# A two-layer decoder step on one core: RMSNorm's factor applied at the PSUM read, split inputs cut chunk by chunk across the norm, prologue by chunks and tail by token tiles

## The chip, the core and the metric

The kernel runs on one core of a Trainium2 chip. TensorE (PE) does matmuls and transposes, VectorE (DVE) and ScalarE (ACT) the work between them, GpSimd (POOL) builds constants and starts some DMAs, SyncE (SP) starts most DMAs. Every engine has its own instruction stream and they meet at semaphores. The metric is the device time of one execution in microseconds (us); lower is better.

## The reference

One inference step of a two-layer trunk for 512 prompt tokens and 64 sample tokens (8 sequences of 8), model width 1024, everything in float32:

```python
def rms_norm(x, g):
    y = xf * lax.rsqrt(jnp.mean(xf * xf, axis=-1, keepdims=True) + EPS) * g
for layer in range(DEPTH):                     # DEPTH = 2
    h = rms_norm(x, g_mix[layer])
    mix = even_mixer(h, ...) if layer % 2 == 0 else odd_mixer(h, ...)
    x = x + mix
    h = rms_norm(x, g_mlp[layer])
    x = x + jnp.square(jax.nn.relu(h @ w_up[layer])) @ w_down[layer]
y = rms_norm(x, g_final)
```

A mixer is one input projection of h, an attention (forgetting in layer 0, stick-breaking in layer 1) beside a gated part, and one output projection. There are five norms: before each mixer, before each MLP, and the last one. The factor `rsqrt(mean)` is one number for each token; the gain `g` is one number for each feature.

## The kernel before

Activations lie feature-major: `X` is 128 partitions x 8 chunks (k) x 576 tokens, so a norm factor is a vector along the free axis, replicated on all partitions in `R` (128x576).

Every projection is cut into **units** of 128 output features. A unit multiplies a 1024x128 weight tile with 576 tokens: 8 chunks k, in each three products (high weight x high input, high weight x low input, low weight x high input; each float32 operand is split into a high part `WH`, `HH` and a low rest `WL`, `HL`), in each two halves of 288 tokens. That is 48 matmuls. Units are numbered through the program (188 of them), alternate between two weight buffers and, before, between PSUM banks 0,1 and 2,3. For unit g, SP loads `WR`, ACT makes `WH` (`cut_high`), DVE makes `WL` (`cut_low`), PE runs `unit`, then ACT and DVE read the banks: `evac_in` copies a projection (ACT one half, DVE the other), `evac_up` takes relu (ACT), squares (DVE), and splits into `ffH` (ACT) and `ffL` (DVE), `evac_add` adds to `X` (DVE), after which ACT squares the chunk and DVE sums it into `SQS`. The tile of a weight buffer can only be cut again when the unit two before has finished, and PE starts a unit only when both readers are done with its banks.

Between the last unit ahead of a norm and the first behind it stands `norm(z)`, z from 0 to 4: PE sums `SQS` over partitions (`rms`), DVE makes mean + EPS in `R`, ACT takes Ln and Exp, DVE multiplies each chunk by gain and `R` into `TMP`, ACT writes `HH`, DVE writes `HL`. `pair_after_norm` runs the first two units behind the norm together, chunk by chunk, as `HL` chunks come:

```python
def scale(k):
    ...
    V.scalar_tensor_tensor(dst, X[:, k, :], gain, R[:], ALU.mult, ALU.mult).then_inc(S["normed"], 1)
```

In the prologue PE waits for POOL's `consts`, transposes `XN` (tokens x features, one DMA) into `X`, and the first norm (z = 0) follows. In the tail (z = 4) the normed `Y` is transposed back in eight steps, copied to `XN` by DVE, and POOL stores it with two DMAs. The order of work on each engine is the order of the program text; there is no scheduler. MLP groups run in the order `MLP_ORDER`: up 0, up 1, down 0, up 2, down 1, up 3, down 2, down 3, eight units each.

Of the kernel before, what the change touches and what calls it, by code (L numbers as in the profile page):

```python
# [19 lines left out]
def trunk(nc, x_prompt, x_sample, cache_fox_k, cache_fox_v, cache_fox_logf, cache_sb_k, cache_sb_v, state_conv,  # L20
# [6 lines left out]
    ds = bass.ds  # L27
# [34 lines left out]
    with ctx:  # L62
# [31 lines left out]
        low_addr = h_addr + KT * T * 4  # L94
        mask_f = place("mask_f", [P, 3, 2, P], F32, low_addr)
# [3 lines left out]
        row_rep = place("row_rep", [2 * NT, NH, 2 * NT], F32, low_addr + 4096)  # L99
        row_neg = place("row_neg", [2 * NT, 2, 2, NT], F32, low_addr + 8192)  # L100
# [18 lines left out]
        ffL = [place(f"ffL{i}", [P, KT, T], F32R, arena + (i * 2 + 1) * KT * T * 4) for i in range(2)]  # L119
        at[0] = arena  # L120
# [64 lines left out]
        def sems(*names):  # L185
            for n in names:
# [4 lines left out]
             "consts", "zeroed", "vec_turned", "x_turned", "x_copied", "x_squared", "x_summed",  # L191
             "sum_step", "rms_sum", "rms_mean", "rms_ln", "rms_scale", "normed", "norm_high", "norm_low",
             "lf_turned", "lf_copied", "lf_suffix_step", "lf_suffixed", "lf_tail", "d_past",
             "wf_high", "wf_low", "f_logits", "f_copied", "f_turned", "f_biased", "f_abs", "f_exp", "f_ln", "f_logf", "F_sums", 
             "nbi_set", "relu_squared", "ff_high",
# [3 lines left out]
             "y_turned", "y_copied", "stored", "stored_kn")  # L199
# [11 lines left out]

        NORM_G = [0, 2 * KT, KT, 3 * KT, 4 * KT]
        CONV_V = 5 * KT

        def unit_loop(eng, body, g0, n, last_plain=False, first_plain=False, i0=0):
# [4 lines left out]
            for u in range(first):  # L220
                body(g0 + u, i0 + u, u, "second" if u == 0 else None)
# [117 lines left out]
        N_STORES = 3 + 2 + 2  # L339
# [7 lines left out]
        def _(sp):  # L347
            sp.dma_start(XN[:, 0:TT, :], x_prompt[0].rearrange("(i p) d -> p i d", p=P)).then_inc(S["x_in"], 16)
            sp.dma_start(XN[0:NS, TT, :], x_sample.rearrange("b t d -> (b t) d")).then_inc(S["x_in"], 16)
            sp.dma_start(pages[0:1, :], page_table.rearrange("(o a) b -> o (a b)", o=1)).then_inc(S["pt_in"], 16)  # L350
            sp.dma_start(vec_rows[0:2 * KT, :], g_mix.rearrange("l (k p) -> (l k) p", p=P)).then_inc(S["vec_in"], 16)
            sp.dma_start(vec_rows[2 * KT:4 * KT, :], g_mlp.rearrange("l (k p) -> (l k) p", p=P)).then_inc(S["vec_in"], 16)
            sp.dma_start(vec_rows[4 * KT:5 * KT, :], g_final.rearrange("(k p) -> k p", p=P)).then_inc(S["vec_in"], 16)
            sp.dma_start(vec_rows[5 * KT:n_vec, :], conv_w[0].rearrange("w (k p) -> (w k) p", p=P)).then_inc(S["vec_in"], 16)
# [18 lines left out]
            for L in range(2):  # L373
# [36 lines left out]
                for kind, grp in MLP_ORDER:  # L410
                    view = up_v[L] if kind == "up" else dn_v[L][grp]
                    unit_loop(sp, load_weights(view, grp * DM if kind == "up" else 0), g, KT)
                    g += KT
            sp.wait_ge(S["stored"], N_STORES * 16)
# [7 lines left out]
        def _(pool):  # L422
            g = nc.gpsimd
            for t in (ident, zero_col, head_rep, step_rep, row_rep, row_neg, mask_f):
                g.memset(t[:], 0.0)
# [3 lines left out]
            pool.wait_ge(S["zeroed"], 1)  # L429
            sel = g.affine_select  # L430

            def step(ins, n=[1]):
# [4 lines left out]
            sel(out=ident[:], in_=ident[:], compare_op=ALU.not_equal, fill=1.0, base=0, pattern=[[-1, P]], channel_multiplier=1)  # L437
# [61 lines left out]
            pool.wait_ge(S["y_copied"], KT)  # L499
            pool.dma_start(y_prompt[0].rearrange("(i p) d -> p i d", p=P), XN[:, 0:TT, :]).then_inc(S["stored"], 16)  # L500
            pool.dma_start(y_sample.rearrange("b t d -> (b t) d"), XN[0:NS, TT, :]).then_inc(S["stored"], 16)
# [5 lines left out]
        def _(act):  # L507
# [32 lines left out]
            def evac_sq(g, i, u, more):  # L540
                next_high(g, u, more)
# [1051 lines left out]
```

## Time and profile before

| | us |
|---|---|
| median of 3 runs | 1721.89 |
| lowest, highest | 1717.29, 1723.42 |
| the profiled execution | 1716.23 |
| its span | 1714.6 |

The times below are from the profiled execution, in microseconds from the start of its span. Its own time is 1.6 us longer than its span and 5.7 us under the median of the runs. PE is busy for 1557.6 us, DVE for 749.6 and ACT for 495.1. A row of the chain names what ended last at each step; a row of the timeline is one group of instructions, with the idle time before it in brackets.

### The profile page before, as it was taken

The numbers are of one execution on the slowest core, as the hardware profiler recorded it, in microseconds if no ns is written. First come the engines' busy times: TensorE is split into PE (matmuls) and PEld (weight loads), VectorE is DVE, ScalarE is ACT, GpSimd is POOL, SyncE is SP. The second block draws the span as 40 slices with busy tenths as digits, with TensorE's granted clock in tenths as the row PEclk, the third lists the DMA queues.
The fourth block names the chain that finished last, engine by engine and source line by source line (L and its number), as shares of the span: only waits on it lengthen the run. The fifth ranks groups of instructions, "written<-read, shape, count | busy, mean of one in ns | idle before, by whom it ended". The sixth has DMA issues, their size and how long they took to land.

```text
span 1714.6 us, 34162 instructions
## 1 busy us (share of the span) xinstructions
PE 1557.6 (91%) x13113; PEld 1453.4 (85%) x13113; DVE 749.6 (44%) x1218; ACT 495.1 (29%) x863; POOL 57.5 (3%) x132
## 2 busy tenths in 40 slices
PE   3999889889799999999979996987979999999994
PEld 2999756569699999999979994655979999999993
DVE  5434446433544343343452355664354433434344
ACT  2221234322333132231232224542233322213120
POOL 4420000000000000000000000000000000000000
PEclk9999989989899999999989998998989999999997
DMA  4232376752122322232222237676112222222221
GB/s 120 66 81 77 109 211 187 227 172 62 50 86 83 89 74 86 79 90 77 86 58 79 85 99 221 179 230 208 57 51 84 79 89 78 86 84 75 88 71 55
DMA packets 239079, 178.74 MB, mean 104 GB/s; under 512 B 9860, under 2 KB 203464, under 8 KB 238986
## 3 DMA queue, kind: packets, MB, share of 16 engines
q1 hardware_dynamic: 234282, 168.62, 33.6%
q0 software_dynamic: 4704, 8.88, 1.6%
q8 instruction: 59, 0.97, 0.2%
q14 instruction: 34, 0.28, 0.1%
HBM read 170.20 MB, written 7.26 MB: 103 GB/s over the span
## 4 chain that ended last, share of the span: by engine, by line
PE 83%; SPq 5%; DVE 4%; issue 3%; ACT 2%; DMA 1%; POOL 1%; POOLq 0%; DVEq 0%; ACTq 0%
PE B L1214 66%; PE B L1229 5%; PE B L1384 2%; SPq L365 2%; SPq L370 2%; PE B L1396 1%; PE B L1478 1%; PE B L1427 1%; PE B L1440 1%; SPq L383 1%; PE B L1416 1%; DVE WL L760 1%; SPq L388 1%; PE B L1273 1%; ACT WH L517 1%
## 5 line engine op out<-in xcount | busy, mean ns | idle before, releaser
L1214 PE MATMUL B<-HH,WH 128*128 128x288 f32 x1792 | 387.5, 298 | 18.6 <-DVE ffL L795 7.9
L1214 PE MATMUL B<-HL,WH 128*128 128x288 f32 x1792 | 385.5, 297 | 0.0
L1214 PE MATMUL B<-HH,WL 128*128 128x288 f32 x1792 | 385.0, 297 | 0.0
L1214 PEld LDWEIGHTS B<-HH,WH 128*128 128x128 f32 x1792 | 291.5, 191 | 20.1 <-ACT TMP L556 8.3
L1214 PEld LDWEIGHTS B<-HL,WH 128*128 128x128 f32 x1792 | 291.6, 191 | 0.0
L1214 PEld LDWEIGHTS B<-HH,WL 128*128 128x128 f32 x1792 | 291.1, 190 | 0.0
L760 DVE TENSOR_TENSOR WL<-WR,WH 128x1024 fp32r<-128x1024 f32 x188 | 230.1, 1224 | 88.6 <-ACT WH L517 48.6
L527 ACT ACTIVATE WH<-WR 128x1024 fp32r<-128x1024 f32 x175 | 184.1, 1052 | 240.5 <-PE B L1214 240.3
L1214 PE MATMUL B<-ffH,WH 128*128 128x288 f32 x1024 | 219.2, 294 | 0.0
L1214 PE MATMUL B<-ffL,WH 128*128 128x288 f32 x1024 | 217.8, 294 | 0.0
L1214 PE MATMUL B<-ffH,WL 128*128 128x288 f32 x1024 | 217.7, 293 | 0.0
L781 DVE TENSOR_TENSOR X<-B,X 128x288 f32 (+1 forms) x160 | 65.8, 453 | 265.3 <-PE B L1214 265.2
L1214 PEld LDWEIGHTS B<-ffL,WH 128*128 128x128 f32 x1024 | 164.7, 187 | 0.0
L1214 PEld LDWEIGHTS B<-ffH,WH 128*128 128x128 f32 x1024 | 163.7, 188 | 0.0
L1214 PEld LDWEIGHTS B<-ffH,WL 128*128 128x128 f32 x1024 | 163.6, 188 | 0.0
L793 DVE TENSOR_TENSOR TMP<-TMP 128x576 f32<-128x576 f32 x64 | 48.5, 758 | 167.9 <-ACT TMP L556 167.9
L556 ACT ACTIVATE TMP<-B 128x288 f32<-128x288 f32 x128 | 45.6, 408 | 198.6 <-PE B L1214 198.6
L1384 PE MATMUL B<-ident,KR 128*128 128x128 f32 x256 | 45.5, 305 | 34.6 <-DMA KR<-in_cache_sb_k_dram 15.0
L795 DVE TENSOR_TENSOR ffL<-TMP,ffH 128x576 f32 (+1 forms) x64 | 48.6, 759 | 61.9 <-ACT ffH L559 61.9
L1384 PEld LDWEIGHTS B<-ident,KR 128*128 128x128 f32 x256 | 29.6, 151 | 45.1 <-issue 35.9
L543 ACT ACTIVATE TMP<-X 128x576 f32 (+1 forms) x32 | 21.9, 685 | 147.7 <-DVE X L781 147.7
L1229 PE MATMUL B<-HH,WH 128*128 128x288 f32 x192 | 46.6, 328 | 19.3 <-DVE HL L820 19.3
(265 smaller groups left out, 1467.0 us busy)
## 6 DMA issues: line engine op xcount, KB each, us to landing
WR<-in_w_up_dram SPq DMA_DIRECT2D x64, 512.0 KB, 4.0
WR<-in_w_down_dram SPq DMA_DIRECT2D x64, 512.0 KB, 3.6
WR<-in_w_in_odd_dram SPq DMA_DIRECT2D x24, 512.0 KB, 3.7
VR<-in_cache_fox_v_dram SPq DMA_DIRECT2D x44, 256.0 KB, 3.1
VR<-in_cache_sb_v_dram SPq DMA_DIRECT2D x44, 256.0 KB, 3.1
WR<-in_w_in_even_dram SPq DMA_DIRECT2D x20, 512.0 KB, 4.0
KR<-in_cache_fox_k_dram SPq DMA_DIRECT2D x32, 256.0 KB, 3.0
KRX<-in_cache_fox_k_dram SPq DMA_DIRECT2D x32, 256.0 KB, 2.9
```

What stands on the lines that cost most here:

```text
L365: v = sp.value_load(pages[0:1, row:row + 1], min_val=0, max_val=POOL - 1)
L370: sp.dma_start(v_slot(n), cache_v[L][0][ds(v, 1)].rearrange("o p h d -> (o p) (h d)")).then_inc(S[f"v_in{n % NV}"], 16)
L527: A(WH[1 - u][:], WR[1 - u][:], ACT.Copy).then_inc(S["w_high"], 1)
L543: A(TMP[:, u, :], X[:, ds(i, 1), :], ACT.Square).then_inc(S["evac_act"], 1)
L556: last = A(TMP[:, u, h * TH:(h + 1) * TH], B[2 * u + h][:, 0:TH], ACT.Relu)
L760: V.tensor_tensor(WL[u][:], WR[u][:], WH[u][:].bitcast(F32), ALU.subtract).then_inc(S["w_low"], 1)
L781: last = V.tensor_tensor(x, B[2 * u + h][:, 0:TH], x, ALU.add)
L793: V.tensor_tensor(TMP[:, u, :], TMP[:, u, :], TMP[:, u, :], ALU.mult).then_inc(S["relu_squared"], 1)
L795: V.tensor_tensor(ffL[grp % 2][:, ds(i, 1), :], TMP[:, u, :].unsqueeze(1), ffH[grp % 2][:, ds(i, 1), :].bitcast(F32), ALU.subtract).then_i ...
L1214: last = M(B[2 * u + h][:, 0:TH], w[u][:, k, :], x[:, k, h * TH:(h + 1) * TH], start=(k == 0 and n == 0), stop=(k == KT - 1 and n == 2))
L1229: last = M(B[2 * u + h][:, 0:TH], w[u][:, k, :], x[:, k, h * TH:(h + 1) * TH], start=(m == 0 and n == 0), stop=(m == KT - 1 and n == 2))
L1384: done = TR(bank[:, c * P:(c + 1) * P], k_slot(n)[:, c * P:(c + 1) * P], ident[:])
```

## The change

The norm factor is no longer applied to the input of the projection but to its result, where PSUM is read: `R` is a factor per token, so it commutes with the product over features (and, being positive, with relu). What the units behind a norm read is then only `X` times the gain, split into high and low, and each chunk of it is cut as soon as that chunk of `X` is final. Five pieces:

1. `split_high` (ACT) and `split_low` (DVE) make the high and low parts in the evacuation of each output unit and each unit of the last down group. Norms 1 and 3 write to a second pair of buffers, `H2H` and `H2L`. `norm(z)` keeps only mean, Ln and Exp.
2. `evac_in` and `evac_up` multiply by `R` on DVE, both halves. ACT no longer reads PSUM there; in `evac_up` it squares `TMP` in place and writes `ffH`.
3. `pair_across` runs the first two units behind a norm in banks 4 to 7, one after the other with chunks 0 to 6, then `rms`, then chunk 7 of both. `two_behind` runs the next two units in banks 0 to 3 without waiting for the evacuation of that pair.
4. Prologue: `x` comes in two column halves, the identity is built first, transposes, copies, splits and the first pair go chunk by chunk, and the mask constants are moved behind the first projection units.
5. Tail: `Y` is `X` times gain, transposed back between the units of the last down group (`turn_y`, `y_natural`); the factor is computed per token as a column and applied to `XN` by token tiles, on DVE and ACT in turn, each stored by SP.

```diff
@@ sync
-            sp.dma_start(XN[:, 0:TT, :], x_prompt[0].rearrange("(i p) d -> p i d", p=P)).then_inc(S["x_in"], 16)
-            sp.dma_start(XN[0:NS, TT, :], x_sample.rearrange("b t d -> (b t) d")).then_inc(S["x_in"], 16)
+            for h in range(2):
+                cols = slice(h * DM // 2, (h + 1) * DM // 2)
+                sp.dma_start(XN[:, 0:TT, cols], x_prompt[0].rearrange("(i p) d -> p i d", p=P)[:, :, cols]).then_inc(S["x_in"], 16)
...
+            for i in (TT, 0, 1, 2, 3):
...
+                    sp.wait_ge(S["y_scaled"], i + 2)
+                    sp.dma_start(y_prompt[0].rearrange("(i p) d -> p i d", p=P)[:, i, :], XN[:, i, :]).then_inc(S["y_stored"], 16)
@@ scalar
             def evac_in(tile_of):
                 def body(g, i, u, more):
                     next_high(g, u, more)
-                    act.wait_ge(S["unit_done"], g + 2)
-                    A(tile_of(i)[:, 0:TH], B[2 * u][:, 0:TH], ACT.Copy).then_inc(S["evac_act"], 1)
+                    act.sem_inc(S["evac_act"], 1)
...
+            def split_high(z, k):
+                gain = vec[:, NORM_G[z] + k:NORM_G[z] + k + 1]
+                if z < 4:
+                    A(H_OF[z][0][:, k, :], X[:, k, :], ACT.Copy, scale=gain).then_inc(S["h_high"], 1)
+                else:
+                    A(Y[:, k, :], X[:, k, :], ACT.Copy, scale=gain).then_inc(S["y_gained"], 1)
...
+                    act.wait_ge(S["evac_dve"], g + 3)
+                    split_high(z, i)
+                    A(TMP[:, u, :], X[:, i, :], ACT.Square).then_inc(S["evac_act"], 1)
+                    if z == 4 and i >= 1:
+                        y_natural(i - 1)
...
-                    for h in range(2):
-                        last = A(TMP[:, u, h * TH:(h + 1) * TH], B[2 * u + h][:, 0:TH], ACT.Relu)
+                    act.wait_ge(S["relu_scaled"], i + (m0 + 1))
+                    A(TMP[:, u, :], TMP[:, u, :], ACT.Square).then_inc(S["relu_squared"], 1)
@@ vector
-                    V.tensor_copy(tile_of(i)[:, TH:T], B[2 * u + 1][:, 0:TH]).then_inc(S["evac_dve"], 1)
+                    for h in range(2):
+                        cols = slice(h * TH, (h + 1) * TH)
+                        done = V.tensor_tensor(tile_of(i)[:, cols], B[b0 + 2 * u + h][:, 0:TH], R[:, cols], ALU.mult)
...
+                V.scalar_tensor_tensor(H_OF[z][1][:, k, :], X[:, k, :], gain, H_OF[z][0][:, k, :].bitcast(F32), ALU.mult, ALU.subtract).then_inc(S["h_low"], 1)
...
-                    V.tensor_tensor(TMP[:, u, :], TMP[:, u, :], TMP[:, u, :], ALU.mult).then_inc(S["relu_squared"], 1)
+                    for h in range(2):
+                        cols = slice(h * TH, (h + 1) * TH)
+                        done = V.scalar_tensor_tensor(TMP[:, u, cols], B[b0 + 2 * u + h][:, 0:TH], 0.0, R[:, cols], ALU.max, ALU.mult)
@@ tensor
+            def pair_across(z, g):
+                for u in range(2):
+                    pe.wait_ge(S["w_low"], g + 3 + u)
+                    for k in range(KT - 1):
+                        pe.wait_ge(S["h_low"], z * KT + k + 1)
+                        chunk(z, g, u, k, k == 0, False)
+                rms(z)
+                pe.wait_ge(S["h_low"], (z + 1) * KT)
+                for u in range(2):
+                    chunk(z, g, u, KT - 1, False, True)
...
+            turn_x(0)
+            turn_x(1)
+            pe.wait_ge(S["consts"], 1)
+            pe.wait_ge(S["w_low"], 4)
+            for k in range(KT):
+                if k + 2 < KT:
+                    turn_x(k + 2)
+                pe.wait_ge(S["h_low"], k + 1)
+                for u in range(2):
+                    chunk(0, 0, u, k, k == 0, k == KT - 1)
+            pe.wait_ge(S["x_copied"], 2 * KT)
+            rms(0)
...
+                            for i in range(KT):
+                                unit(ffH[grp % 2], ffL[grp % 2])(g + i, i, i % 2, None)
+                                if i >= 1:
+                                    turn_y(i - 1)
```

On PE, at the norm before the MLP of layer 0, this is the order before: the last matmuls of the output projection, the row sum over `SQS`, then the two units of the pair taking turns chunk by chunk (`WH_55`, `WL_57` are the tiles of one weight buffer, `WH_56`, `WL_58` of the other).

```order
L1214 MATMUL B<-HH,WH_56 128x288 x2
L1214 MATMUL B<-HL,WH_56 128x288 x2
L1214 MATMUL B<-HH,WL_58 128x288 x2
L223 REGISTER_ALU
L223 COMPARE_AND_BRANCH
L1240 MATMUL B<-SQS,ones 128x288 x2
L1229 MATMUL B<-HH,WH_55 128x288 x2
L1229 MATMUL B<-HL,WH_55 128x288 x2
L1229 MATMUL B<-HH,WL_57 128x288 x2
L1229 MATMUL B<-HH,WH_56 128x288 x2
```

The same place of the change, at its row sum: ahead of it is the seventh chunk of the pair's second unit, behind it the eighth chunk of both units, and then (L1264) the next unit.

```order
L1296 MATMUL B<-H2H,WH_56 128x288 x2
L1296 MATMUL B<-H2L,WH_56 128x288 x2
L1296 MATMUL B<-H2H,WL_58 128x288 x2
L1304 MATMUL B<-SQS,ones 128x288 x2
L1296 MATMUL B<-H2H,WH_55 128x288 x2
L1296 MATMUL B<-H2L,WH_55 128x288 x2
L1296 MATMUL B<-H2H,WL_57 128x288 x2
L1296 MATMUL B<-H2H,WH_56 128x288 x2
L1296 MATMUL B<-H2L,WH_56 128x288 x2
L1296 MATMUL B<-H2H,WL_58 128x288 x2
L1264 MATMUL B<-H2H,WH_55 128x288 x2
```

So 84 of the pair's 96 matmuls have moved ahead of the row sum, and 12 stand behind it.

On PE, the end of the program before: the row sum, then eight times a set of five transposes of `Y` (two sets shown; the rest repeat).

```order
L1240 MATMUL B<-SQS,ones 128x288 x2
L1563 MATMUL B<-ident,Y 128x128 x4
L1564 MATMUL B<-ident,Y 64x128
L1563 MATMUL B<-ident,Y 128x128 x4
L1564 MATMUL B<-ident,Y 64x128
```

The same place of the change, from the last matmuls of the last unit on: six sets already stand between the units of the last group, two are left, and five narrow products make the token sums.

```order
L1264 MATMUL B<-ffH_86,WH_56 128x288 x2
L1264 MATMUL B<-ffL_88,WH_56 128x288 x2
L1264 MATMUL B<-ffH_86,WL_58 128x288 x2
L1274 MATMUL B<-ident,Y 128x128 x4
L1275 MATMUL B<-ident,Y 64x128
L1274 MATMUL B<-ident,Y 128x128 x4
L1275 MATMUL B<-ident,Y 64x128
L1659 MATMUL B<-ones,SQS 128x1 x4
L1659 MATMUL B<-ones,SQS 64x1
```

The transposes have moved ahead of the row sum, and the row sum itself has become narrow.

## Rows read from the trace of the kernel before

**Rows 1.** The page: the span, and engines' busy time, share and instructions.
```profile
span 1714.6 us, 34162 instructions
PE 1557.6 (91%) x13113; PEld 1453.4 (85%) x13113; DVE 749.6 (44%) x1218; ACT 495.1 (29%) x863; POOL 57.5 (3%) x132
```

**Rows 2.** The chain that ended last, prologue: start, us, what.
```profile
14.76 1.04 PE B L1255 x4
...
41.08 14.93 PE B L1229 x90
56.09 1.07 ACT WH L517
...
58.92 38.61 PE B L1214 x288
```

**Rows 3.** The chain at the norm before the MLP of layer 0.
```profile
429.93 7.74 PE B L1214 x58
...
440.30 2.30 PE B L1240 x4
...
442.62 0.83 DVE R L803 x2
...
447.39 14.87 PE B L1229 x90
...
463.43 1.23 DVE WL L760
...
466.98 8.05 PE B L1214 x48
```

**Rows 4.** Timeline, PE's last matmuls ahead of the norm of layer 1's mixer.
```profile
861.17 0.42 PE L1214 MATMUL B<-ffH,WL 128*128 128x288 f32 x2
```

**Rows 5.** The chain: the unit behind that norm, and the norm before layer 1's MLP.
```profile
886.71 76.70 PE B L1214 x576
...
1249.93 8.15 PE B L1214 x61
...
1286.32 395.49 PE B L1214 x2976
```

**Rows 6.** The chain in layer 0's output projection, behind its first pair.
```profile
395.79 0.69 ACT TMP L543
396.53 41.14 PE B L1214 x288
```

**Rows 7.** Stretches: length, busy time by engine, granted TensorE clock, DMA share, GB/s.
```profile
466.98:470.44 3.46, 3.46 (x14) 3.46 (x15) 2.51 (x3) 1.64 (x2) 0.00 (x0) 0.51 0.37 112
...
58.92:62.00 3.08, 3.08 (x23) 3.08 (x24) 1.35 (x2) 0.00 (x0) 1.14 (x4) 1.00 0.79 178
```

**Rows 8.** One stretch of the prologue, same columns.
```profile
15.00:16.00 1.00, 1.00 (x5) 0.58 (x3) 0.96 (x10) 0.00 (x0) 0.00 (x0) 1.00 0.30 72
```

**Rows 9.** Groups by line and shape: busy us, mean ns, idle before.
```profile
L811 DVE SCALAR_TENSOR_TENSOR TMP<-X,vec,R 128x576 f32<-128x576 f32 x32 | 25.8, 818 | 4.3 <-ACT R L567 3.4
...
L781 DVE TENSOR_TENSOR X<-B,X 128x288 f32 x148 | 60.9, 453 | 258.8 <-PE B L1214 258.8
...
L1119 DVE TENSOR_SCALAR SP__123<-SP__123,stat 128x1088 f32<-128x1088 f32 x4 | 3.1, 787 | 0.1
```

**Rows 10.** Groups by line on ACT, the same columns.
```profile
L543 ACT ACTIVATE TMP<-X 128x576 f32 x26 | 17.8, 686 | 130.2 <-DVE X L781 130.2
```

**Rows 11.** Timeline of the tail; the last column is idle time before.
```profile
1681.37 0.42 PE L1214 MATMUL B<-ffH,WL 128*128 128x288 f32 x2
...
1699.36 0.63 PE L1563 MATMUL B<-ident,Y 128*128 128x128 f32 x4
...
1703.13 0.55 POOL L501 DMA_DIRECT2D out_dram<-XN  x1
```

**Rows 12.** DMA issues: KB each, us from issue to landing.
```profile
WR<-in_w_in_even_dram SPq DMA_DIRECT2D x20, 512.0 KB, 4.0
...
out_dram<-XN POOLq DMA_DIRECT2D x1, 256.0 KB, 7.5
```

More of the change, by code:

```diff
@@ L743, in _ @@
                     last = L == 1 and n == len(MLP_ORDER) - 1
-                    body = evac_up(L, grp) if kind == "up" else evac_sq if grp == FG - 1 else evac_none
-                    unit_loop(act, body, g, KT, last, n == 0)
-                    g += KT
-            norm(4)
+                    if kind == "down" and grp == FG - 1:
+                        for i in range(KT):
+                            evac_sq(2 + 2 * L)(g + i, i, i % 2, None if last and i == KT - 1 else "next")
+                    else:
+                        unit_loop(act, evac_up(L, grp) if kind == "up" else evac_none, g, KT, first_plain=n == 0)
+                    g += KT
+            y_natural(KT - 1)
+            rt = small[:, 0:TT + 1]
+            act.wait_ge(S["tok_mean"], 1)
+            A(rt, rt, ACT.Ln).then_inc(S["tok_ln"], 1)
+            act.wait_ge(S["tok_ln"], 1)
+            A(rt, rt, ACT.Exp, scale=-0.5).then_inc(S["tok_scale"], 1)
+            act.wait_ge(S["tok_scale"], 1)
+            act.wait_ge(S["y_scaled"], 2)
+            A(XN[:, 1, :], XN[:, 1, :], ACT.Copy, scale=small[:, 1:2]).then_inc(S["y_scaled"], 1)
+            act.wait_ge(S["y_scaled"], 4)
+            A(XN[:, 3, :], XN[:, 3, :], ACT.Copy, scale=small[:, 3:4]).then_inc(S["y_scaled"], 1)
         @block.vector
@@ L844, in _ @@
                 else:
-                    dve.wait_ge(S["x_summed"], k)
-                    V.tensor_tensor(SQS[:], SQS[:], TMP[:, k % 2, :], ALU.add).then_inc(S["x_summed"], 1)
-            cut_low(0, 0)
-            cut_low(1, 1)
+                    V.tensor_tensor(SQS[:], SQS[:], TMP[:, k % 2, :], ALU.add).then_inc(S["sum_step"], 1)
+                if k in (0, 1):
+                    cut_low(k, k)
             norm(0)
@@ L1180, in _ @@
                 V.memset(SQS[:], 0.0)
-                unit_loop(dve, evac_add(True), G_OUT[L], KT, first_plain=True)
                 dve.wait_ge(S["stored_v"], 32 * (L + 1))
+                for i in range(KT):
+                    evac_add(1 + 2 * L)(G_OUT[L] + i, i, i % 2, "second" if i == 0 else None if i == 1 else "next")
                 cut_low(G_MLP[L] + 1, 1)
@@ L1217, in unit, with turn_y @@
                 return body
+            def turn_y(k):
+                pe.wait_ge(S["y_gained"], k + 1)
+                if k >= 2:
+                    pe.wait_ge(S["y_copied"], k - 1)
+                for i in range(TT):
+                    TR(B[4 + 2 * (k % 2)][:, i * P:(i + 1) * P], Y[:, k, i * P:(i + 1) * P], ident[:])
+                TR(B[5 + 2 * (k % 2)][0:NS, 0:P], Y[:, k, NP:T], ident[:]).then_inc(S["y_turned"], 1)
             def first_pair(g, order, wait):
@@ L1232, in first_pair, with chunk, rms @@
                             last.then_inc(S["unit_done"], 1)
-            def pair_after_norm(z, g):
-                first_pair(g, range(KT), lambda k: pe.wait_ge(S["norm_low"], z * KT + k + 1))
-            def rms(z, name, value):
-                pe.wait_ge(S[name], value)
+            def chunk(z, g, u, k, first, last):
+                hi, lo = H_OF[z]
+                for n, (w, x) in enumerate(((WH, hi), (WH, lo), (WL, hi))):
+                    for h in range(2):
+                        done = M(B[4 + 2 * u + h][:, 0:TH], w[u][:, k, :], x[:, k, h * TH:(h + 1) * TH],
+                                 start=(first and n == 0), stop=(last and n == 2))
+                if last:
+                    done.then_inc(S["unit_done"], 1)
+            def rms(z):
+                pe.wait_ge(S["sum_step"], (z + 1) * KT)
                 for h in range(2):
```

235 lines of the change are left out of this document (128 added, 107 removed).

## The prediction

> **What bounds the kernel now.** The page comes first: of the 1714.6 us span PE is busy for 1557.6, DVE for 749.6 and ACT for 495.1 [rows 1]. So PE is the bound nearly everywhere, and only what PE executes, or what it stands idle for, is worth anything. The long stretches have no hole: in the last MLP, 62 units of 48 matmuls run in 395.49 us [rows 5], which is 6.38 us a unit and 0.133 us a matmul. No part of the change touches that rate. The chain of waits comes next, read at the five norms. At the norm before layer 0's MLP, the last matmul of the output projection ends at 429.93 + 7.74 = 437.67, and the third unit behind the norm starts at 466.98 [rows 3]: 29.3 us for two units, which at full rate are 12.8. In between stand the row sum (2.30), the mean (0.83), Ln and Exp, scaling and splitting of the first chunk up to 447.39, the pair at 14.87, and then a weight cut and the pair's evacuation. The norm before layer 1's MLP takes 1258.08 to 1286.32, 28.2 us [rows 5]; that of layer 1's mixer from 861.17 + 0.42 = 861.59 [rows 4] to 886.71 [rows 5], 25.1 us. In the prologue the transposes start at 14.76, the pair at 41.08 and the third unit at 58.92 [rows 2]. In the tail the last matmul ends at 1681.37 + 0.42 = 1681.79 and the span at 1714.6, 32.8 us later [rows 1, 11]. The windows give the clock: behind the 4.3 us idle ahead of 466.98 the granted clock is 0.51 for 3.46 us, which is the 1.2 GHz level, while behind the 2.1 us idle ahead of 58.92 it is 1.00 [rows 7].
>
> **The three inner norms.** Let T be the end of the last unit. Chunks 0 to 6 are already split, so PE goes straight on: 84 matmuls, 11.2 us. Meanwhile, for chunk 7, DVE adds (2 x 0.45 [rows 9]), ACT makes the gained chunk and its square (2 x 0.69 [rows 10]), DVE splits (0.82) and sums; some 4 us, hidden. The second weight buffer's cut (1.07 and 1.23 [rows 2, 3]) comes out by about T + 5, ahead of the second unit at T + 5.6. Then comes the row sum. It took 2.30 at half clock [rows 3]; PE has now been busy, so I take half, 1.2: T + 12.4. Behind it PE has 12 matmuls (1.6), but the third unit waits longer, for this queue: mean 0.83 on DVE, Ln and Exp on ACT (2 x 0.69, as wide as the row in [rows 10]), and, behind them in ACT's own order, the cut of the third unit's weights, 1.07, then 1.23 on DVE, plus 0.2 for hops. That is 4.75, so the third unit starts at T + 17.15, after 3.1 us of idle PE. What is late next is the fourth unit's weight in the MLPs: DVE and ACT evacuate both units of the pair first (for each: two reads at 0.45, square and copy at 0.69, subtraction), and only then cut; I get T + 24.85 against the third unit's end at T + 23.5, or at T + 25 if the clock has fallen. So 1.3 to 1.5 us goes either way, as it does before, where the half-clock stretch costs about 1.5. I set these equal. Gains: 29.3 - 17.15 = 12.2, 28.2 - 17.15 = 11.1, 25.1 - 17.15 = 8.0; together 31.3.
>
> The 3.1 us idle lies between 2.1 (clock kept) and 4.3 (clock fallen) [rows 7]; I take the nearer price above, a fall, at each. The clock costs nothing or 1.5 at each place, so up to 4 us of gain stay in the range. The Trainium skill (TensorE: Matmul & The Clock Gate, section Why this matters for your kernels) says that idle gaps between bursts of matmuls send the clock back to its lower level. By that rule the fall is charged at each norm, as my sum does; by the row at 58.92 alone it would not be, and the time would be some 3 to 4 us shorter.
>
> **Prologue.** All loads were in by 15.3 [rows 8], with the spare weight tile last. I put the first tile at 13 and the second at 15 (an estimate from that end and 4.0 us for a tile [rows 12]). ACT then cuts (1.07), does chunk 1 (three passes of 0.69), and cuts again (1.07), and DVE follows (1.23): PE may start chunks at 18.6. From there PE has six sets of transposes (0.63 for four at full clock [rows 11]; 0.7 a set), 96 matmuls (12.8), and the half-clock start, which in the pair before cost 14.93 - 90 x 0.133 = 3.0 [rows 2]: 38.6. ACT needs some 2.2 us a chunk and PE 2.3, so PE is the longer by a hair. Row sum 1.2, mean 0.83, Ln and Exp 1.4; then ACT cuts the forget tile (1.07) and the third unit's (1.07) and DVE the latter (1.23), hops 0.2: start at 45.6. Six us of idle lower the clock, 2 us. Gain 58.9 - 45.6 - 2 = 11.3. If the weight tiles land as late as 20, 5 less.
>
> **Tail.** Behind the last matmul: add 0.9, `Y` chunk and square 1.4, sum 0.8; token sums, two narrow means, Ln and Exp on five columns, together an estimated 1.9; then four tile passes in series and one for the sample rows, 0.8 on DVE for 1088 columns [rows 9] and 1.07 on ACT for 1024 [rows 2]: 0.8 + 0.6 + 1.1 + 0.8 + 1.1. The last store is issued near T + 9.5. The store before took from 1703.13 to 1710.6 by its 7.5 us [rows 11, 12], and 4.0 passed to the end; a 512 KB tile on SP's queue I put at 4.0 as for a weight tile [rows 12], bounded above by 7.5. End at T + 17.5 at most 21. From 32.8 that is 15.5 saved, less the six sets of transposes now ahead of T, 6 x 0.7 = 4.2 (four transposes took 1.04 in the prologue [rows 2], so a set might cost 1.3; with PE busy ahead of them I don't expect that): 11.3.
>
> **What it costs.** In both output projections ACT now makes the split ahead of the square, and PE's third unit waits for that square (395.79 + 0.69, PE at 396.53 [rows 6]): 0.7 each, 1.4. Where transposes wait for an evacuation, DVE reads both halves (0.9 for 0.46): 0.4 at three places, 1.2. The mask product moves behind the first units: 0.3 on PE; its 2.5 us on DVE lie under the forget gate's product, 48 matmuls or 6.4 us, and if that cover were gone they would cost 2. In the steady units the reads on DVE cost nothing: cut 1.23, two reads 0.9, subtraction 0.76 make 2.9 of 6.38 us, and the whole chain from a unit's end to the next weight is 4.7. Cover: the unit that runs. Costs: 2.9.
>
> **Sum**: 31.3 + 11.3 + 11.3 - 2.9 = 51.0. The profiled execution's 1716.2 becomes 1665.2. The median of the runs lies 5.7 above that execution, so on its scale I forecast 1671.
>
> **Rivals.** *A, the forecast*: gain 40 to 62, time 1660 to 1682. Chance 0.60. *B, the wait moves to the weight cut*: PE no longer waits for the scaled input, but for the tile cut queued behind Ln and Exp. For it: ACT and DVE have no other order. Against: my sum of it is only 4.75. If the idle is 6 instead of 3.1 and the clock costs 1.5 more at three norms, 13.5 is lost: 1684. Chance 0.20. *C, the prologue or the tail yields nothing*, since weights land behind `x` or the stores complete no sooner: 11 less, 1682. Chance 0.10. *D, more than forecast*: the clock stays up, stores overlap, 1652 to 1659. Chance 0.05. *E, slower*: DVE becomes the bound of the MLP and projection units. The place is DVE's read of PSUM in `evac_up`; the chain from a unit's end through two reads, square, copy, two cuts and subtraction is 4.7 us by the rows, and decides from 6.38 on. It would have to reach 6.38 + 51/128 = 6.8 us a unit over the 128 units of the MLPs to eat the gain, at 7.0 us the time would be 1671 + 0.62 x 128 = 1750. Against it: 453 ns for a two-operand read of PSUM, 148 times in this very kernel [rows 9]. Chance 0.03. *F, nothing moves*, because PE waits at the head of the pair for a chunk that is split late, so that the pair still begins behind the norm: 1715 to 1722. Against it: chunks 0 to 6 are final 6.4 us before. Chance 0.02.
>
> The Trainium skill (VectorE: DVE Perf Modes, section The TRN2 errata) speaks for E: it prices a PSUM read on VectorE above one on ScalarE, for 288 columns 425 against 383 ns by its formulas. The trace agrees on VectorE, 453 ns, and at that price E's chain stays under its point.
>
> **The numbers.** The median of three runs spans 0.36%, so about 0.5% (8.6 us) is what this kernel's measurement can tell from no change. The range takes in A, B and C and some of D: 1654 to 1693. Faster by over 0.5%: A to D, 0.95. Within: F, 0.02. Slower: E, 0.03.
>
> **What the profile would show.** PE runs on without a gap from the last unit before each inner norm into the pair, and `SQS`'s row sum stands 11.2 us behind it. The only idle of PE is then about 3 us ahead of the third unit, and about 1 ahead of the fourth in the MLPs, ended by `WL`. In the prologue PE starts chunks near 18.6 and the third unit near 45.6. The tail from the last matmul is near 17.5 us. The MLP units stay at 6.38 us. I am wrong if idle ahead of the third unit is 5 us or more, if PE waits for `TMP` or `ffL` inside the groups, if the prologue's pair is broken by waits for `HL`, or if the stores take over 7 us.

## The result, and the profile after

| | before | after |
|---|---|---|
| median of 4 runs each, us | 1722.60 | 1668.63 |
| lowest, highest | 1717.29, 1723.42 | 1666.99, 1669.54 |
| ratio, 95% interval | | 0.9692 [0.9671, 0.9713] |
| profiled execution, its span | 1716.23, 1714.6 | 1666.99, 1665.3 |

The change makes the kernel 3.1% faster. The time lies 2.4 us under the forecast of 1671, and the spans differ by 49.3 us where the sum said 51.0. That agreement hides misses of opposite sign, as the ledger below shows.

The page after, to be held against [rows 1]: PE is busy for 15 us less, and its share has risen from 91 to 93%; DVE and ACT are no busier than before.

```profile
span 1665.3 us, 33771 instructions
PE 1542.4 (93%) x13119; PEld 1445.1 (87%) x13119; DVE 729.8 (44%) x1267; ACT 493.6 (30%) x787; POOL 57.9 (3%) x130
```

The chain after (start, us, what), at the three inner norms, for [rows 3 to 5]. Each has the same picture: 84 matmuls in 11.1 us, the row sum (four matmuls), 12 matmuls, an idle of 3.1 (`issue` is time in which PE waited for nothing that the profile shows), and the third unit. Not every row is shown at every norm.

```profile
433.32 11.10 PE B L1296 x84
...
445.39 1.58 PE B L1296 x12
...
446.97 3.09 issue
...
450.06 395.27 PE B L1264 x2976
...
845.32 11.19 PE B L1296 x84
...
859.08 3.08 issue
...
862.15 77.02 PE B L1264 x576
...
1234.07 11.10 PE B L1296 x84
...
1245.17 0.97 PE B L1304 x4
...
1250.81 358.26 PE B L1264 x2688
```

The span splits at places that both kernels have. T is the end of the last unit ahead of a norm, and the last column what the prediction's terms give for the stretch. The column sums to 50.8, not 51.0: by the prediction's own end at T + 17.5 the tail saves 32.8 - 17.5 = 15.3, where it says 15.5.

| stretch | before | after | gained | forecast |
|---|---|---|---|---|
| start to the first QKV unit | 111.23 | 110.16 | 1.1 | 10.6 |
| to T of norm 1 | 326.4 | 323.2 | 3.3 | -1.1 |
| norm 1, T to third unit | 29.31 | 16.74 | 12.6 | 12.2 |
| to T of norm 2 | 394.6 | 395.3 | -0.6 | 0 |
| norm 2 | 25.12 | 16.83 | 8.3 | 8.0 |
| to T of norm 3 | 371.4 | 371.9 | -0.6 | -1.1 |
| norm 3 | 28.24 | 16.74 | 11.5 | 11.1 |
| to the last matmul of the last unit | 395.5 | 399.7 | -4.2 | -4.2 |
| tail, to the end of the span | 32.8 | 14.8 | 18.0 | 15.3 |

The norms and the MLPs are right within half a microsecond each. The prologue brought a tenth of its forecast; the stretch behind it (4.4 better than forecast) and the tail (2.7) made up for most of that.

The timeline of PE in the prologue after, idle time in brackets, for [rows 2]. The first three rows are where the prediction put them (chunks at 18.6, third unit at 45.6). The last is the miss.

```profile
18.82 1.09 PE L1334 MATMUL B<-ident,XN 128*128 128x128 f32 x4 [7.73 <-issue]
...
39.03 1.13 PE L1304 MATMUL B<-SQS,ones 128*128 128x288 f32 x4
...
45.97 0.82 PE L1264 MATMUL B<-HH,WH 128*128 128x288 f32 x2 [5.81 <-issue]
...
94.69 1.14 PE L1373 MATMUL B<-ident,lf_raw 64*128 64x64 f32 x8 [7.21 <-DMA lf_raw<-in_cache_fox_logf_dram]
```

PE arrives 10.0 us earlier than before at the transposes of the forget gate's cache (87.5 against 97.5), and then stands for 7.2 us: the rows of that cache come one by one over GpSimd's queue. The chain has the landing, the late transposes and the forget gate's product:

```profile
92.25 2.39 DMA lf_raw<-in_cache_fox_logf_dram
94.69 1.14 PE B L1373 x8
95.83 8.21 PE B L1381 x48
...
110.16 4.93 PE B L1264 x37
```

GpSimd's last load of a row, in the timeline, is issued at 92.25, and in the kernel before at 89.49 (next two rows, after and before). It has hardly moved; PE has.

```profile
92.25 0.49 POOL L480 DMA_DIRECT2D lf_raw<-in_cache_fox_logf_dram  x1 [0.65 <-issue]
```

```profile
89.49 0.48 POOL L463 DMA_DIRECT2D lf_raw<-in_cache_fox_logf_dram  x1 [0.68 <-issue]
```

The windows after (length, busy time by engine, granted clock, DMA share, GB/s) give what the clock did: in the prologue's third unit, in the forget gate's product, and behind the equal idles at norms 1, 2 and 3.

```profile
45.97:51.80 5.83, 5.83 (x24) 5.83 (x25) 2.50 (x5) 0.00 (x0) 2.43 (x5) 0.51 0.69 180
...
95.83:104.04 8.21, 8.21 (x49) 8.21 (x50) 2.13 (x9) 0.60 (x1) 0.00 (x0) 0.78 0.00 0
...
450.06:453.00 2.94, 2.94 (x16) 2.94 (x17) 1.47 (x4) 1.37 (x2) 0.00 (x0) 0.67 0.48 134
...
862.15:865.00 2.85, 2.85 (x21) 2.85 (x22) 2.50 (x5) 0.00 (x0) 0.00 (x0) 1.00 0.51 150
...
1250.81:1253.50 2.69, 2.69 (x11) 2.69 (x12) 1.23 (x3) 1.36 (x2) 0.00 (x0) 0.50 0.40 109
```

In the prologue this makes a full account. The third unit stands 12.95 us earlier (58.92 to 45.97). From there to PE's arrival at the cache it takes 41.5 us, 38.6 before: 2.9 given back, nearly all to the half clock. The wait takes 7.2, the eight transposes 0.1, the forget product 1.7 (8.21 against 6.54, at a mean clock of 0.78 behind the wait). What is left is 1.1.

### The profile page after: what moved, and what is told of

It is laid out like the page before. It is cut to its first block, busy times and chain, and to the rows that moved or that the text cites. A ratio compares the mean times of both kernels' runs of the same rounds, so it can differ in the third digit from the quotient of the medians.

```text
span 1665.3 us, 33771 instructions
## 1 busy us (share of the span) xinstructions
PE 1542.4 (93%) x13119; PEld 1445.1 (87%) x13119; DVE 729.8 (44%) x1267; ACT 493.6 (30%) x787; POOL 57.9 (3%) x130
## 3 DMA queue, kind: packets, MB, share of 16 engines
q8 instruction: 64, 1.05, 0.3%
## 4 chain that ended last, share of the span: by engine, by line
PE 81%; SPq 5%; issue 5%; DVE 2%; DMA 2%; POOLq 2%; POOL 1%; ACT 1%; DVEq 0%; ACTq 0%
PE B L1264 66%; PE B L1477 3%; PE B L1296 2%; SPq L372 2%; SPq L377 2%; PE B L1489 2%; PE B L1287 1%; POOLq L479 1%; PE B L1571 1%; PE B L1520 1%; PE B L1533 1%; PE B L1509 1%; POOL lf_raw L480 1%; SPq L390 1%; PE B L1364 1%
## 5 line engine op out<-in xcount | busy, mean ns | idle before, releaser
L1264 PE MATMUL B<-ffH,WH 128*128 128x288 f32 x1024 | 219.7, 295 | 0.0
L1264 PE MATMUL B<-ffL,WH 128*128 128x288 f32 x1024 | 218.0, 294 | 0.0
L1264 PE MATMUL B<-ffH,WL 128*128 128x288 f32 x1024 | 217.5, 293 | 0.0
L1264 PE MATMUL B<-H2H,WH 128*128 128x288 f32 x960 | 207.6, 297 | 6.2 <-issue 6.2
L1264 PE MATMUL B<-H2L,WH 128*128 128x288 f32 x960 | 206.0, 296 | 0.0
L1264 PE MATMUL B<-H2H,WL 128*128 128x288 f32 x960 | 205.3, 295 | 0.0
L1264 PE MATMUL B<-HH,WH 128*128 128x288 f32 x832 | 182.2, 301 | 16.8 <-issue 8.9
L1264 PE MATMUL B<-HL,WH 128*128 128x288 f32 x832 | 180.9, 300 | 0.0
L1264 PE MATMUL B<-HH,WL 128*128 128x288 f32 x832 | 180.6, 299 | 0.0
L1264 PEld LDWEIGHTS B<-ffL,WH 128*128 128x128 f32 x1024 | 164.6, 187 | 0.0
L1264 PEld LDWEIGHTS B<-ffH,WL 128*128 128x128 f32 x1024 | 163.7, 187 | 0.0
L1264 PEld LDWEIGHTS B<-ffH,WH 128*128 128x128 f32 x1024 | 163.4, 188 | 0.0
L1264 PEld LDWEIGHTS B<-H2H,WH 128*128 128x128 f32 x960 | 154.8, 190 | 6.6 <-issue 6.6
L1264 PEld LDWEIGHTS B<-H2L,WH 128*128 128x128 f32 x960 | 156.2, 189 | 0.0
L1264 PEld LDWEIGHTS B<-H2H,WL 128*128 128x128 f32 x960 | 154.9, 189 | 0.0
L1264 PEld LDWEIGHTS B<-HH,WH 128*128 128x128 f32 x832 | 136.7, 193 | 18.1 <-issue 9.5
L1264 PEld LDWEIGHTS B<-HL,WH 128*128 128x128 f32 x832 | 136.7, 192 | 0.0
L1264 PEld LDWEIGHTS B<-HH,WL 128*128 128x128 f32 x832 | 136.7, 192 | 0.0
```

The lines of the kernel that those rows point to most:

```text
L1264: last = M(B[2 * u + h][:, 0:TH], w[u][:, k, :], x[:, k, h * TH:(h + 1) * TH], start=(k == 0 and n == 0), stop=(k == KT - 1 and n == 2))
```

## The experiments

Ratios are to the kernel before, run on the same chip beside the variant; its medians were 1718.3, 1720.2 and 1720.2 on the three chips used. One hundredth of a ratio is 17.2 us. The spread of a variant's runs is up to 13 us (18 in `before_gather12`), so a difference between two variants is read from ratios and, where it is small, from the place in the profile.

### The forget cache's rows: is the 7.2 us wait the whole of the prologue's miss?

The theory: the queue of 64 row loads is what ate the gain, and where it is shortened, the early start comes out at the end. The rival: something else is late next (weights, mask constants), so that nothing comes out. Half of the rows move to SyncE, behind the loads of the third and fourth weight tile, in the changed kernel and in that of before, where the same loads should be hidden.

```diff
+                for u in range(2):
+                    load_weights(in_v[L], side + 2 * P)(G_IN[L] + 2 + u, u, u, None)
+                if L == 0:
+                    sp.wait_ge(S["pt_in"], 16)
+                    for q in range(NB * PG // 2, NB * PG):
+                        v = sp.value_load(pages[0:1, q:q + 1], min_val=0, max_val=POOL - 1)
+                        sp.dma_start(lf_raw[q:q + 1, :, :], cache_fox_logf[0][ds(v, 1)]).then_inc(S["lfp_sp"], 16)
@@ pool
-            for q in range(NB * PG):
+            for q in range(NB * PG // 2):
```

Expected of it in the changed kernel:

> The changed kernel, with half of the 64 row loads of the forget-gate cache moved from GpSimd's queue to SyncE's, behind the loads of the third and fourth weight tile. Theory: the prologue's gain was eaten by GpSimd's row loads, which end at 94.6 us and for which PE, now early, waits 7.2 us, with a half-clock stretch of 1.7 behind it. Then 8 to 9 us go: about 1660. Rival: behind that wait stands another (the suffix sums, with the mask work now ahead of them on DVE), so that at most 2 us go: 1666 to 1668.

Expected of it in the kernel before:

> The kernel before, with the same half of the row loads on SyncE's queue. Theory: there the loads ended at 91 and PE came for them at 97.5, so they are hidden: within 1.5 us of the kernel before. Rival: the loads on GpSimd's queue cost something by themselves (contention, slow queue), then this kernel too gains 5 us or more.

Measured: 0.9704 [0.9671, 0.9737] in the changed kernel, no gain; 1.0091 [1.0056, 1.0126] in that of before, 15 us slower. Both expectations were missed. PE no longer waits for the cache, but for a weight. The timeline of SyncE's queue in the changed kernel and in the kernel before with this edit:

```profile
20.20 39.64 SPq L392 DMA_DIRECT2D lf_raw<-in_cache_fox_logf_dram  x32
...
60.20 65.78 SPq L366 DMA_DIRECT2D WR<-in_w_in_even_dram  x10
```

```profile
37.82 39.71 SPq L385 DMA_DIRECT2D lf_raw<-in_cache_fox_logf_dram  x32
```

And the waits of the kernel before with this edit (us in all, times, longest):

```profile
PE B L1221 <- DVE WL L767: 12.2, 1, 12.2
```

Each row load holds SyncE for 1.24 us, far more than I had reckoned, and the loads of the next weights stand behind them. So the experiment exchanged one queue's delay for another's and told nothing of the theory. The next version, `gather12`, moves fewer rows: 12 of 64, some 14 us of GpSimd's queue, which is about twice what PE waited, and 15 of SyncE's.

```diff
-                    for q in range(NB * PG // 2, NB * PG):
+                    for q in range(NB * PG - 12, NB * PG):
@@ pool
-            for q in range(NB * PG // 2):
+            for q in range(NB * PG - 12):
```

> The changed kernel, with 12 of the 64 row loads on SyncE's queue instead of 32. A row load takes 1.24 us of SyncE, so 32 held the queue for 39.6 us and the fifth unit's weight came late; 12 hold it for 15, to about 35, ahead of any need. GpSimd's part then ends near 80, ahead of PE at 87. Theory: the wait of 7.2 us goes and nothing takes its place, and the forget product runs at full clock (6.5 for 8.2 us): 1659 to 1661. Rival: the suffix sums or the transposes behind them become the wait: 1664 or more.

> The kernel before, with 12 of the 64 row loads on SyncE's queue, which holds it from 37 to 52 us, ahead of the fifth unit's need at about 60. Theory: in the kernel before the row loads were hidden (last one at 91, PE there at 97.5), so no change: within 2 us. Rival: the row loads cost there too, then 5 us or more faster.

Measured: 0.9641 [0.9625, 0.9657], that is 0.0051 or 8.8 us under the change, and 0.9984 [0.9968, 1.0000] in the kernel before, 2.7 us by the ratio and 1.9 in the median. So the same edit brings the kernel before, which doesn't wait for the rows, little or nothing. The chain of the changed kernel with this edit:

```profile
86.86 0.33 PE B L1375 x2
87.19 1.02 PE B L1381 x8
88.22 6.54 PE B L1389 x48
...
100.88 11.19 PE B L1271 x84
```

The wait is gone, nothing has taken its place, and the forget product is back at 6.54. The first QKV unit starts at 100.88 instead of 110.16: 9.3 us, which is the prologue's miss (9.5) and about the gain in the median (9.9). Both theories hold, and this settles the cause.

### What the 3.1 us idle ahead of the third unit is made of

The prediction put this idle down to the queue "mean, Ln and Exp, then the weight cut". If so, it is nearly halved when ACT cuts the third unit's weights ahead of Ln and Exp, and DVE ahead of its wait for them. If it were the row sum itself, nothing would change. The edit of `unit_loop` takes the same cut out of its old place behind Ln and Exp.

```diff
@@ unit_loop
-                (ahead or body)(g0 + u, i0 + u, u, "second" if u == 0 else None)
+                (ahead or body)(g0 + u, i0 + u, u, None)
@@ scalar
+                if z < 4:
+                    cut_high(G_AFTER[z] + 2)
                 act.wait_ge(S["rms_mean"], z + 1)
                 A(R[:], R[:], ACT.Ln)
@@ vector
+                cut_low(G_AFTER[z] + 2, 0)
                 V.memset(SQS[:], 0.0)
                 dve.wait_ge(S["rms_scale"], z + 1)
```

> The changed kernel with the cut ahead of Ln and Exp alone. Theory: in the prologue the third unit starts up to 2.5 us earlier but PE then waits for GpSimd's row loads that much longer, so only the three inner norms count: 1.1 to 1.4 us each, and clock: 3 to 5 us, about 1664.5. Rival: it brings as much as on top of gather_sp, 6 to 7: 1662.

> gather12 with the third unit's weight cut ahead of Ln and Exp, as in gather_cut, which was 6.7 under gather_sp. Theory: the two edits touch different waits and add: 5 to 7 under gather12, 1652 to 1656. Rival: in the prologue the time that the cut saves is lost at the gather's own next wait (it ends at a fixed time): 2 to 4 under gather12 only.

> gather_sp and, in each norm, the cut of the third unit's weights ahead of Ln and Exp on ACT and ahead of the wait for R on DVE. Theory: the 3.1 us of idle PE ahead of the third unit is the cut queued behind Ln and Exp; ahead of them it leaves 1.6 to 2.0, so 1.1 to 1.4 at each of three inner norms, and 1.4 to 2.5 in the prologue, and the clock falls less often: 5 to 9 us under gather_sp, about 1653. Rival: the clock falls regardless and the fourth unit's weights, which wait for the evacuation, are late by as much: 0 to 2 us.

Measured: `cut_first` 0.9676 [0.9653, 0.9700], 2.8 us by the ratio and 5.2 in the median under the change; the intervals overlap, so what it is worth is read from the rows. With 12 rows on SyncE as well, `gather12_cut` is 0.9600 [0.9577, 0.9622], 7.0 by the ratio and 9.1 in the median under `gather12`. With 32 rows, `gather_cut` is 0.9680 [0.9654, 0.9706], 4 by the ratio and 6.7 in the median under `gather_sp`, also with overlapping intervals; its 1653 was missed with `gather_sp`'s 1660. Timeline of PE in `cut_first`, the third and fourth unit behind norm 1, and the cache's transposes:

```profile
451.41 0.51 PE L1268 MATMUL B<-H2H,WH 128*128 128x288 f32 x2 [1.72 <-issue]
...
459.25 0.54 PE L1268 MATMUL B<-H2H,WH 128*128 128x288 f32 x2 [1.25 <-DVE WL L802]
```

```profile
94.54 0.70 PE L1377 MATMUL B<-ident,lf_raw 64*128 64x64 f32 x4 [13.78 <-DMA lf_raw<-in_cache_fox_logf_dram]
```

The idle falls from 3.09 to 1.72, as the queue theory has it. What is left is the cut itself, which now starts when the pair's first unit is done with the buffer, as the timeline of ACT and DVE in `cut_first` shows (PE goes on at 451.41):

```profile
448.99 1.06 ACT L532 ACTIVATE WH<-WR 128x1024 fp32r<-128x1024 f32 x1 [9.77 <-PE B L1300]
...
450.08 1.23 DVE L802 TENSOR_TENSOR WL<-WR,WH 128x1024 fp32r<-128x1024 f32 x1 [1.12 <-ACT WH L532]
```

The fourth unit's weight is now late by 1.25, which the prediction had as the next thing. The clock stayed up behind this idle at all three norms (1.00 in each third unit). In the prologue the third unit comes 4 us earlier (41.8), but the wait for the cache grows from 7.2 to 13.8 and takes nearly all of it: the first QKV unit starts at 109.69 instead of 110.16. With 12 rows on SyncE the cut pays: in `gather12_cut` the first QKV unit starts at 96.8, 4.1 before that of `gather12`, although PE is now early enough to wait for the rows again, a little:

```profile
81.53 1.09 PE L1385 MATMUL B<-ident,lf_raw 64*128 64x64 f32 x8 [1.45 <-DMA lf_raw<-in_cache_fox_logf_dram]
```

It is the best version, 1649.64 us, 19 under the change.

### Which part of the change pays at the norms?

The pieces at a norm are three: the factor is applied at the PSUM read, the pair runs across the row sum, and the third and fourth unit don't wait for the pair's evacuation. `row_sum_first` undoes the second alone.

```diff
             def pair_across(z, g):
+                rms(z)
                 for u in range(2):
                     ...
-                rms(z)
                 pe.wait_ge(S["h_low"], (z + 1) * KT)
```

> The changed kernel, with the row sum ahead of the whole pair instead of ahead of its last chunk. Theory: what a norm gains comes mostly from taking the factor out of the input, and the crossing saves only the wait for the sum: PE stands 3.4 us at each inner norm and the third unit starts 2.4 to 3.5 later, with some half clock; 7 to 13 us in all: 1676 to 1682. Rival: the crossing is the main part of the gain: 8 us or more a norm, 1693 or more.

`row_first_wait` undoes the third as well, so that the factor at the PSUM read stands alone.

```diff
-unit(hi, lo, 2)(g + u, u, u, None)
+unit(hi, lo, 0)(g + u, u, u, None)
```

> The changed kernel, with the row sum ahead of the pair, and the third and fourth unit waiting for the pair's evacuation. What is left at the inner norms is the factor at the PSUM read alone. Theory: in the MLPs the third unit then waits 3 us more for the first unit's evacuation (read, square, copy, subtraction), and the fourth some, at the mixer's norm 1 us: 6 to 9 above row_sum_first. Rival: evacuation of the pair is hidden beneath the weight cut anyway: 0 to 2 above row_sum_first.

Measured: 0.9766 [0.9733, 0.9798], 12.7 us by the ratio and 9.9 in the median above the change, and 0.9801 [0.9783, 0.9820], another 6 (8.1 in the median). Both lie where the theories put them. The chain of `row_sum_first` at norm 1, T at 433.15:

```profile
433.19 0.83 DVE X L828 x2
...
436.39 1.27 PE B L1304 x4
437.66 14.20 PE B L1296 x96
451.86 1.79 issue
453.65 395.27 PE B L1264 x2976
```

PE stands for the row sum's input (3.2 us) and runs all 96 matmuls behind it, so the third unit is at T + 20.5 instead of 16.7. The chain of `row_first_wait`, T at 433.43, ends in the pair's evacuation instead:

```profile
451.44 1.07 ACT WH L531
452.60 1.23 DVE WL L799
453.83 0.74 DVE TMP L844 x2
...
456.02 0.77 DVE ffL L847
456.92 395.89 PE B L1264 x2976
```

That is T + 23.5. The third unit's start behind T, in us, at all three norms, and what each piece brings (the factor at the PSUM read, the free banks, the crossing):

| | before | `row_first_wait` | `row_sum_first` | change | factor | banks | crossing |
|---|---|---|---|---|---|---|---|
| norm 1 | 29.3 | 23.5 | 20.5 | 16.7 | 5.8 | 3.0 | 3.8 |
| norm 2 | 25.1 | 19.8 | 19.0 | 16.8 | 5.3 | 0.8 | 2.2 |
| norm 3 | 28.2 | 24.6 | 19.0 | 16.7 | 3.7 | 5.6 | 2.2 |

So of the 32.4 us at the norms the factor at the PSUM read brings 14.8, the free banks 9.4 and the crossing 8.2. The split at one norm holds some luck of the clock. The row sum took 2.30 us before at norm 1 and 1.24 at norm 3, in `row_first_wait` 1.24 and 2.29, which is 1.05 in favour of the factor at norm 1, and at norm 3 1.05 against it and for the banks. The pair of `row_sum_first` took 14.20 at norm 1 and 12.78 at norm 2, so 1.4 of the 3.8 is clock. The sums over the norms are the safer reading.

### Does the doubled PSUM read on DVE cost anything?

Rival E lives if DVE is close to its bound in the up groups. Two more PSUM reads of 256 columns for each up unit, written to a tile that nothing reads any more, add 0.84 us of DVE between the unit's end and its evacuation.

```diff
+                    for h in range(2):
+                        V.scalar_tensor_tensor(dump[:, h * 256:(h + 1) * 256], B[b0 + 2 * u + h][:, 0:256], 0.0, R[:, 0:256], ALU.max, ALU.mult)
                     for h in range(2):
                         cols = slice(h * TH, (h + 1) * TH)
                         done = V.scalar_tensor_tensor(TMP[:, u, cols], ...)
```

> The changed kernel; in every up unit DVE reads both PSUM banks once more (256 of 288 columns, result unused), some 0.8 us more of DVE for each of 64 units. Theory: DVE's reads in the steady units lie under the unit that PE runs: 0 to 3 us more, and only behind the two MLP norms. Rival: DVE is near the bound in up units, and 0.8 us on 64 units shows: 20 us or more.

Measured: 0.9695 [0.9671, 0.9720], no change. The groups of that run (busy us, mean ns, idle before) show both the doubled and the needed reads, 128 times each:

```profile
L847 DVE SCALAR_TENSOR_TENSOR TMP<-B,R 128x288 f32<-128x288 f32 x128 | 52.0, 448 | 0.0
...
L844 DVE SCALAR_TENSOR_TENSOR D_past<-B,R 128x256 f32<-128x256 f32 x128 | 48.3, 419 | 79.0 <-PE B L1267 79.0
```

Rival E is out with 0.84 us an up unit to spare. The price of the read, 448 ns here and 452 in the change, was the 453 assumed from [rows 9]. By a formula of the Trainium skill (VectorE: DVE Perf Modes, section The TRN2 errata) a PSUM read of 288 columns comes to 425 ns, an estimate. The rows are 5 to 6% above it.

### What in the tail pays: the queue or the tiles?

`pool_store` issues the five final stores on GpSimd instead of SyncE; nothing else is changed. `one_store` leaves them on SyncE but stores the prompt's 512 tokens by one DMA when all four tiles are scaled; the sample rows' store waits for the tiles too and is issued 0.6 us ahead of it (1658.70 and 1659.30), so 0.6 of its cost is this order.

```diff
@@ sync
-            for i in (TT, 0, 1, 2, 3):
+            sp.wait_ge(S["y_scaled"], 5)
...
+            sp.dma_start(y_prompt[0].rearrange("(i p) d -> p i d", p=P), XN[:, 0:TT, :]).then_inc(S["y_stored"], 16)
```

> The changed kernel, with the five final stores started by GpSimd instead of SyncE. Theory: the queue counts for little beside the order of the work; the last store then takes 1 to 3 us longer: 1669.5 to 1672. Rival: most of what the tail gained in storing (5.0 us from last issue to the end, against 11.5 before) is the queue: 5 us or more.

> The changed kernel, with the prompt's output stored by a single DMA once all tiles are scaled. Theory: the token tiles pay because three of four stores are done before the last tile: one store of 2 MB needs some 3 to 4 us more: 1671.5 to 1673. Rival: stores in parts land no earlier than one: within 1 us.

Measured: 0.9728 [0.9707, 0.9749] and 0.9732 [0.9710, 0.9754], 6.2 and 6.9 us by the ratio above the change (5.5 and 4.6 in the medians). In the profiled executions, both end 13.5 us behind the first scaled tile's start, the change 9.6, so 3.9 is the part that stands at the place itself. For `one_store` this was expected, and its store's landing shows it; the DMA issues of `one_store`, of `pool_store` and of the change (KB each, us to landing):

```profile
out_dram<-XN SPq DMA_DIRECT2D x1, 2048.0 KB, 7.8
```

```profile
out_dram<-XN POOLq DMA_DIRECT2D x4, 512.0 KB, 4.1
```

```profile
out_dram<-XN SPq DMA_DIRECT2D x4, 512.0 KB, 4.3
```

For `pool_store` it was not: the rival, that the queue is worth 5 us or more, is nearer. On GpSimd the stores land as soon as on SyncE (4.1 against 4.3, medians of four), but the span ends 8.6 us after the last one is issued (1663.21 to 1671.8), which is 4.5 after it has landed. In the change the last store can be issued at the earliest when its tile is scaled, at 1660.34, and the span ends 5.0 later, 0.7 behind a landing of 4.3. The last 7.8 of `one_store` ends at 1667.1, 0.4 ahead of its end. What passes on GpSimd's side in those 4 us isn't in the trace and stays open.

## Why the prediction was right, and where it was wrong

**The inner norms**, forecast 31.3, measured 32.4. Each step is there: PE runs from the last unit into the pair without a gap, the row sum stands 11.1 us behind T, the idle is 3.09, 3.08 and 3.09 (forecast 3.1), and the third unit is at T + 16.74, 16.83 and 16.74 (17.15). `cut_first` shows that the idle is the queue of Ln, Exp and weight cut. Rival B, the same mechanism at twice the size, is out.

**The clock at the norms.** I charged a fall behind each idle. It fell in two of three, behind idles of 3.08 and 3.09: at norm 3 from the third unit's first matmul (0.50), at norm 1 some 0.9 us later (0.67 in the mean of 2.94 us), and at norm 2 not at all (1.00). The Trainium skill's rule that gaps between bursts of matmuls send the clock down (TensorE: Matmul & The Clock Gate, section Why this matters for your kernels) held at two places and not at the third. The prediction's reading of the rows was too simple as well. The idle ahead of 466.98 is 3.94 us in the timeline, not 4.3, and the kernel before has a second idle of 2.1, ahead of norm 2's third unit, behind which the clock did fall (0.50 from 888 to 890 us):

```profile
886.71 0.71 PE L1214 MATMUL B<-HH,WH 128*128 128x288 f32 x2 [2.12 <-DVE PB L772]
```

So idles of 2.1 and of 3.1 us each went both ways here, and "2.1 keeps, 4.3 loses" was no rule.

**The late weight of the fourth unit**, which I set equal to what a fall costs, is there but smaller than my 1.3. In `gather_sp`, whose norms are those of the change, the clock stayed up behind norm 1, and the fourth unit waited 0.71:

```profile
454.08 0.51 PE L1271 MATMUL B<-H2H,WH 128*128 128x288 f32 x2 [3.09 <-issue]
...
461.38 0.53 PE L1271 MATMUL B<-H2H,WH 128*128 128x288 f32 x2 [0.71 <-DVE WL L806]
```

Where the clock fell, in the change and in `gather12`, the slow third unit covers that wait. From the third unit to the next T it took 394.7 us in `gather_sp`, 395.3 in the change and 396.3 in `gather12`. A fall thus costs 0.6 to 1.6 us more than none, not nothing. The kernel before fell there too, so its 394.6 doesn't price the fall.

**The prologue**, forecast 11.3 less its share of the costs, measured 1.1. The step that failed is "Gain 58.9 - 45.6 - 2 = 11.3". The places in it were right within half a microsecond, and the clock cost 2.9 instead of 2; but the line takes the whole of an earlier start as gain without asking what the program meets next that comes at its own time. The forget gate's cache was that: before, its last row was issued at 89.49 and, if it took the 2.4 us of the chain's row, had landed only 5.6 us ahead of PE; PE then came 10.0 earlier and the row 2.8 later, which makes the wait of 7.2. The prediction named GpSimd's queue nowhere in this part. Rival C had the outcome in this stretch, no gain, but by another cause, late weights, and at a time, 1682, that didn't come. `gather12`, which takes the wait away, gives 9.3 us back.

**The tail**, forecast 15.3 behind the last matmul, measured 18.0. The term that was off is the end of the stores: I let 4.0 us pass between the last landing and the end, from the store before. That store was GpSimd's, and `pool_store` shows that this wait comes with its queue (4.5 there); on SyncE it is 0.7. The other two terms were a little short: the last tile is scaled at T + 9.9 (9.5) and its store lands in 4.3 (4.0). The transposes between the units cost 4.2, as forecast.

**The costs**, forecast 2.9. In the output projections the third unit starts 4.76 us behind the pair, 4.02 before (forecast 0.7 more). PE's waits of the change (us in all, times, longest) hold these two places in one row, 4.0 each, where before it was 6.5 in all:

```profile
PE B L1264 <- ACT TMP L565: 7.9, 2, 4.0
```

**What stays open** is the 3.3 us gained between the first QKV unit and T of norm 1, where I forecast 1.1 lost. The same stretch took 326.4 us before and 323.2 after, but also 327.5 in `gather12`, 324.1 in `gather12_cut`, 326.3 in `cut_first` and 328.9 in `gather_sp`, which have no edit in it, and 329.4 in `before_gather12`. So single executions scatter by 5 us there, and the 3.3 is not shown to be a gain of the change. Against before, the change's execution waited 1.2 us less for the attention's cache loads (14.1 for 15.3) and PE was busy 2.6 us less (292.4 for 295.1, at a mean granted clock of 0.94 and 0.93), while its other waits grew by 0.8 (16.7 for 15.9), of the kind that I forecast. Why clock and loads differ from one execution to the next isn't shown.

The number 1671 came out right within 2.4 us in part by luck. In the spans a miss of -9.5 met +4.4 and +2.7, which leaves the profiled execution 1.8 us above its 1665.2. The 5.7 us that I added to reach the median were 1.6 in the change (1668.63 against 1666.99), which turned that into 2.4 under. By its own terms it was right at the norms, in the MLPs and in the costs, and wrong by a factor of ten in the prologue.

## What to carry to other kernels

Where a stretch is started earlier, follow every queue to the next point at which it meets the bounding engine, and write down how much slack each has now: a load that landed 6 us ahead of its reader takes back whatever is gained beyond those 6. A row load whose address comes from a register cost its issuing queue over 1 us here, for only 4 KB, so such loads are to be dealt out between queues by counts: moving 12 of 64 paid 9 us, and moving 32 paid nothing. Behind a norm, cut the next unit's weights ahead of the small operations that wait for the row sum, and put the last stores on SyncE.

## What the runs showed of the hardware

- A 4 KB row load with an address from a register took 1.24 us of SyncE's time (32 in 39.64 us). On GpSimd such loads followed each other by 1.12 to 1.17 us, but for two of 1.45.
- Idles of 3.08 to 3.09 us of PE left the granted clock at 1.00, 0.67 and 0.50 in one execution. Behind an idle of 2.13 in the kernel before (58.92) it was 1.00, behind one of 2.12 (886.71) it fell to 0.50. Behind the idles of 1.72 and 1.73 in `cut_first` it was 1.00 at all three norms, and behind 1.79 in `row_sum_first` it fell at one norm of three (0.61 in the mean from 453.65).
- After the last store was issued, the span ended 8.6 us later on GpSimd's queue and about 5 on SyncE's, though both kinds of 512 KB store landed within 4.3 us in the median.
- Four fp32 transposes take 0.60 to 0.66 us between matmuls at full clock and 1.09 to 1.11 at the start of the prologue.
- A read of 128x288 fp32 in PSUM on VectorE with a second operand took 448 to 453 ns, and one of 128x256 took 419.
